# Final stage of a mixture-of-experts step: last block's act turned earlier, other blocks' sums added on TensorE, tiles normed one by one

## The reference

```
moe_ffn(h):      top_w, top_idx = softmax(top_4(h @ w_router + b_router))
                 for each block of up to 128 tokens of one expert:
                     g = min(h @ w_gate + b_gate, 7);  u = clip(h @ w_up + b_up, -7, 7)
                     a = (u + 1) * g * sigmoid(1.702 * g)
                     f[token] += top_w * (a @ w_down + b_down)
layer:           x = x + gate2 * f            (gate2: one row for the prompt, one per sample sequence)
output:          y = x * rsqrt(mean(x**2) + 1e-6) * g_final
```

## Time and profile before

| | |
|---|---|
| median of 3 runs (lowest, highest) | 1815.8 us (1811.48, 1818.57) |
| the profiled execution's own time | 1816.97 us |
| its span in the trace | 1815.2 us |
| TensorE busy | 1680.0 us, 93% of the span, 9012 instructions |
| VectorE busy | 1429.5 us, 79% |
| ScalarE busy | 1106.6 us, 61% |
| POOL busy | 330.1 us, 18% |
| moved by DMA | 516.08 MB, mean 284 GB/s |

### The profile page before, as it was taken

One profiled execution on the slowest core, in us unless ns is written; L12 is line 12 of the kernel. 1 busy time (PEld: TensorE's weight loads), 2 busy tenths in 40 slices (PEclk: granted clock), 3 DMA queues, 4 the chain that ended last, 5 costly groups with the idle time before them and its releaser, 6 DMA issues.

```text
span 1815.2 us, 27011 instructions
## 1 busy us (share of the span) xinstructions
PE 1680.0 (93%) x9012; PEld 1305.1 (72%) x9012; DVE 1429.5 (79%) x1357; ACT 1106.6 (61%) x1060; POOL 330.1 (18%) x310
## 2 busy tenths in 40 slices
PE   3999978788998779999999999999999999999994
PEld 2776767555554468888888888888888888888873
DVE  4422572576425879999999999999999999999996
ACT  4222342454434367777777777777777777777772
POOL 0000121300101012123122222312222231231110
PEclk9999989699998689999999999999999999999997
DMA  9454452610226479999999999999999999999973
GB/s 345 178 186 165 98 169 84 222 80 20 74 74 197 180 260 347 385 372 378 369 379 376 373 377 376 373 374 378 380 371 381 374 373 383 378 378 368 384 288 124
DMA packets 114598, 516.08 MB, mean 284 GB/s; under 512 B 25870, under 2 KB 47710, under 8 KB 62058
## 3 DMA queue, kind: packets, MB, share of 16 engines
q1 hardware_dynamic: 101082, 483.48, 70.6%
q0 software_dynamic: 12800, 29.45, 5.8%
q10 hardware_dynamic: 656, 2.36, 0.3%
HBM read 502.75 MB, written 31.09 MB: 294 GB/s over the span
## 4 chain that ended last, share of the span: by engine, by line
PE 61%; DVE 2%; ACT 1%; DMA 1%; issue 0%; DVEq 0%; POOL 0%; ACTq 0%; POOLq 0%
PE banks L2949 57%; PE banks L2957 3%; PE banks L2935 1%; DMA ffn_rows<-weighed,block_rows 0%; DVE arena L3220 0%; DVE arena L3219 0%; ACT sigmoids L3121 0%; DVE split L3142 0%; PE banks L3000 0%; ACT split L3053 0%; DMA arena<-ffn_rows 0%; DVE arena L3238 0%; DVEq L2816 0%; ACT final_stat L3122 0%; ACT L3127 0%
## 5 line engine op out<-in xcount | busy, mean ns | idle before, releaser
L2949 PE MATMUL banks<-split 128*128 128x512 f32 x4608 | 1077.3, 393 | 6.9 <-DVE split L3146 5.8
L2949 PEld LDWEIGHTS banks<-split 128*128 128x128 f32 x4608 | 861.2, 189 | 192.1 <-issue 13.2
L3142 DVE TENSOR_TENSOR split<-expert_buffers,split 128x2048 fp32r<-128x2048 f32 x384 | 864.4, 2284 | 41.4 <-ACT split L3053 39.8
L3053 ACT ACTIVATE split<-expert_buffers 128x2048 fp32r<-128x2048 f32 x384 | 732.9, 1918 | 217.7 <-PE banks L2949 213.3
L2888 POOL TENSOR_TENSOR wait_taken<-routing 128x1 f32<-128x1 f32 x62 | 76.5, 1234 | 808.9 <-PE banks L2957 464.1
L2911 POOL DMA_INDIRECT ffn_rows<-weighed,block_rows x31 | 107.7, 3476 | 4.8 <-issue 4.8
L662 PE MATMUL banks<-w_in_high,hT_high 128*128 128x476 f32 x192 | 75.6, 394 | 4.2 <-DVE hT_low L498 4.2
L3146 DVE TENSOR_TENSOR split<-banks,split 128x1024 fp32r<-128x1024 f32 x64 | 77.8, 1216 | 0.7 <-ACT split L3056 0.7
L662 PE MATMUL banks<-w_in_high,hT_low 128*128 128x476 f32 x192 | 72.9, 380 | 0.0
L3056 ACT ACTIVATE split<-banks 128x1024 fp32r<-128x1024 f32 x64 | 64.5, 1007 | 4.3 <-PE banks L2957 4.3
L3078 ACT ACTIVATE weighed<-banks,block_weights 128x1024 f32<-128x1024 f32 x32 | 35.8, 1117 | 45.3 <-PE banks L2949 45.3
(11 more groups left out here) (398 smaller groups left out, 1721.2 us busy)
## 6 DMA issues: line engine op xcount, KB each, us to landing
expert_buffers<-in_w_gate SPq DMA_DIRECT2D x128, 1024.0 KB, 8.0
expert_buffers<-in_w_up SPq DMA_DIRECT2D x128, 1024.0 KB, 18.9
expert_buffers<-in_w_down SPq DMA_DIRECT2D x128, 1024.0 KB, 8.5
arena<-in_w_ada SPq DMA_DIRECT2D x16, 1024.0 KB, 4.8
w_in_landing<-in_w_in SPq DMA_DIRECT2D x5, 1904.0 KB, 7.9
arena<-in_w_ada SPq DMA_DIRECT2D x4, 2048.0 KB, 20.6
arena<-in_x_prompt SPq DMA_DIRECT2D x8, 512.0 KB, 9.7
arena<-in_cache_cmp SPq DMA_DIRECT2D x32, 128.0 KB, 2.9
```

The source lines that it names most:

```text
L2949: last = pe.matmul(ps[:, bank + c, :], x[:, kt * P:(kt + 1) * P].bitcast(F32R), wt.bitcast(F32R), start=(m == 2 and kt == 0 and x is xs[0] ...
L3053: act.activation(high[:, j % RING_Q].bitcast(F32R), v, ACT.Copy).then_inc(s_high, 1)
L3142: dve.tensor_tensor(rest[:, j % RING_Q].bitcast(F32R), v, high[:, j % RING_Q], ALU.subtract).then_inc(s_rest, 1)
```

## The change

Five things change, all in `experts`:

1. **Act 31 is turned between the second and third quarter of down(30)** instead of behind it. Its split goes into `xh`, `xl`, ahead of the later quarters in ScalarE's and VectorE's queues, and down(31) writes the banks `GB` instead of `DB`.
2. **POOL takes the last block's rows and weights early**, into tiles of their own, before its last two adds. `hot` no longer waits for the add of block 30.
3. **TensorE adds the loaded sums**: for the four prompt tiles two float32 products with the identity matrix follow those with `hot`, in the same banks. The sample tile's sums are added by VectorE. The products with `hot` take `last_y` as it is; gate2 comes afterwards, once for each tile.
4. **The tiles are finished one by one**: Sqrt by ScalarE for a tile, reciprocal by VectorE, and one VectorE operation for scale and `g_final`. Ln, Exp and the two tiles of ScalarE are gone.
5. **Each tile is stored as soon as it is finished**, in the order 4, 0, 1, 2, 3.

```diff
@@ SP
-            for i, t in enumerate((FINAL[4], FINAL[0], FINAL[3], FINAL[1], FINAL[2])):
+            for i, t in enumerate(FINAL):
                 t0, n = TILES[t]
-                sp.wait_ge(s_oa if t in BY_ACT else s_o, i // 2 + 1)
+                sp.wait_ge(s_o, i + 1)
@@ POOL, behind the loop
+            pool.tensor_tensor(last_row, core.row_of[:, bass.ds(nb1, 1)], none, ALU.add).then_inc(s_lastrow, 1)
+            pool.tensor_tensor(last_weight, core.weight_of[:, bass.ds(nb1, 1)], none.bitcast(F32), ALU.add).then_inc(s_lastrow, 1)
             for n, done in ((nb2, nb3), (nb1, nb2)):
                 take_row(n, done)
                 add_rows(n, done)
-            take_row(nb, nb1)
@@ TensorE
-                product(2, (ah, al), DB, before)
+                product(2, (ah, al), DB, before, range(2))
+                if last:
+                    pe.wait_ge(s_a, nb)
+                    turn(u, s_atp)
+                product(2, (ah, al), DB, before, range(2, 4))
...
-            pe.wait_ge(s_a, nb)
-            turn(u, s_atp)
-            down(nb, nb1, first_of(nb1))
+            pe.wait_ge(s_at, nb)
+            product(2, (xh, xl), GB, first_of(nb1))
...
+            def other_rows(t):
+                pe.wait_ge(s_f[t], 16)
+                for c in range(2):
+                    last = pe.matmul(ps[:, BANK[t] + c, :], ident, f[:, t, c * 512:(c + 1) * 512], start=False, stop=True)
+                return last
 
             pe.wait_ge(s_hot, NT)
             pe.wait_ge(s_y, nb)
-            last_rows(ST, y)
-            pe.wait_ge(s_yg, 1)
+            last_rows(ST).then_inc(s_last, 1)
             for t in range(ST):
                 if t == 3:
                     pe.wait_ge(s_read, 1)
-                last_rows(t, yg)
+                last_rows(t)
+                other_rows(t).then_inc(s_last, 1)
@@ ScalarE
+            def weigh_last():
+                act.wait_ge(s_used, first_of(nb1) + 4)
+                act.wait_ge(s_lastrow, 2)
+                act.activation(last_y, ps[:, GB:GB + 2, :].rearrange("p b n -> p (b n)"), ACT.Copy, scale=last_weight
+                               ).then_inc(s_y, 1)
...
-                for j in range(3):
+                high_part(0, k)
+                if last:
+                    act.wait_ge(s_atp, nb)
+                    rounded(xh, s_ah)
+                for j in range(1, 3):
                     high_part(j, k)
...
-            link(act.activation(row, one, ACT.Ln))
+            link(act.activation(row, one, ACT.Sqrt))
             for i, t in enumerate(FINAL):
                 n = TILES[t][1]
                 act.wait_ge(s_x, i + 1)
                 link(act.activation(junk[0:n, :], x[0:n, t, :], ACT.Square, accum_out=stat[0:n, t:t + 1]))
-                act.activation(stat[0:n, NT + t:NT + t + 1], stat[0:n, t:t + 1], ACT.Ln, scale=1.0 / D,
-                               bias=eps[0:n, :]).then_inc(s_ln, 1)
...
+                act.activation(stat[0:n, NT + t:NT + t + 1], stat[0:n, t:t + 1], ACT.Sqrt, scale=1.0 / D, bias=eps[0:n, :]
+                               ).then_inc(s_rms, 1)
@@ VectorE
-                for j in range(4):
+                rest_part(0, k)
+                if last:
+                    rest_T(xh, xl, s_ah, nb, s_at)
+                for j in range(1, 4):
                     rest_part(j, k)
...
+            def sum_up(i, t):
                 n = TILES[t][1]
+                ft, gate = f[0:n, t, :], gate2[0:n, int(t == ST), :]
+                if t == ST:
+                    dve.wait_ge(s_f[ST], 16)
+                    dve.tensor_tensor(ft, ft, added(i, t), ALU.add).then_inc(s_read, 1)
+                    dve.wait_ge(s_read, 1)
+                    link(dve.tensor_tensor(ft, ft, gate, ALU.mult))
+                else:
+                    link(dve.tensor_tensor(ft, added(i, t), gate, ALU.mult))
+                dve.tensor_tensor(x[0:n, t, :], x[0:n, t, :], ft, ALU.add).then_inc(s_x, 1)
+
+            def finish(i, t):
+                n = TILES[t][1]
+                rstd = stat[0:n, NT + t:NT + t + 1]
+                dve.wait_ge(s_rms, i + 1)
+                link(dve.reciprocal(rstd, rstd))
+                dve.scalar_tensor_tensor(f[0:n, t, :], x[0:n, t, :], rstd, gfin[0:n, :], ALU.mult, ALU.mult).then_inc(s_o, 1)
...
             for i, t in enumerate(FINAL):
+                sum_up(i, t)
+                if i == 1:
+                    dve.wait_ge(s_gf, 16)
+                if i >= 1:
+                    finish(i - 1, FINAL[i - 1])
+            finish(NT - 1, FINAL[NT - 1])
```

More of the change, by code:

```diff
@@ L2768, in experts @@
     row_out, weight_out = own("block_rows", 1).bitcast(I32), own("block_weights", 1)
+    last_row, last_weight = own("last_block_rows", 1).bitcast(I32), own("last_block_weights", 1)
     g, u, s, y = (own(name, D) for name in ("gates", "ups", "sigmoids", "weighed"))
@@ L2785, in experts @@
     f = Stack(core, core.z_late, ARENA - N_SPLIT).take(NT * D).rearrange("p (t d) -> p t d", t=NT)
-    gfin, hot, junk, yg = xg, g[:, 0:NTOK], s, u
-    stat, row, rowf, rowt = own("final_stat", 2 * NT), own("ln_before", 1), own("last_rows", 1), own("last_rows_by_tile", NT)
+    gfin, hot, junk, last_y = xg, g[:, 0:NTOK], u, s
+    stat, row, rowf, rowt = own("final_stat", 2 * NT), own("root_loaded", 1), own("last_rows", 1), own("last_rows_by_tile", NT)
     FINAL = [ST] + list(range(ST))
-    BY_ACT = FINAL[0:2]
     BANK = {ST: GB, 0: UB, 1: TB, 2: DB, 3: GB}
     s_f = [core.sem(f"sums_in{t}") for t in range(NT)]
[L2792 to L2796, removed]
+    s_gf, s_hot, s_last, s_read = (core.sem(n) for n in (
+        "g_final_in", "last_rows_marked", "last_rows_ps", "last_rows_read"))
+    s_x, s_rms, s_o, s_out, s_act = (core.sem(n) for n in (
+        "x_final", "root_mean_square", "out_ready", "out_stored", "act_p7"))
+    s_lastrow = core.sem("last_block_taken")
     s_sum = [core.sem("gather_allowed"), core.sem("add_allowed")]
@@ L2935, in start_with_bias, with product @@
                     pe.matmul(ps[:, bank + c, :], ones[r0:r0 + 3, :], bias[r0:r0 + 3, :], start=True, stop=False)
-            def product(m, xs, bank, before):
-                for q in range(4):
+            def product(m, xs, bank, before, some=range(4)):
+                for q in some:
                     j = 4 * m + q
@@ L2984, in turn_act, with down @@
                 turn(u, s_atp)
-            def down(n, done, before):
+            def down(n, done, before, last=False):
                 pe.wait_ge(s_at, n)
@@ L3018, in step @@
                     turn_rows(k + 1)
-                down(k, prev, first_of(prev) + 8)
+                down(k, prev, first_of(prev) + 8, last)
             step(1, 0)
@@ L3024, in _, with last_rows @@
             step(nb1, nb2, last=True)
-            pe.wait_ge(s_a, nb)
-            turn(u, s_atp)
-            down(nb, nb1, first_of(nb1))
-            def last_rows(t, src):
+            pe.wait_ge(s_at, nb)
+            product(2, (xh, xl), GB, first_of(nb1))
+            def last_rows(t):
                 t0, n = TILES[t]
                 for c in range(2):
-                    last = pe.matmul(ps[0:n, BANK[t] + c, :], hot[:, t0:t0 + n], src[:, c * 512:(c + 1) * 512], start=True, stop=True)
-                last.then_inc(s_last, 1)
+                    last = pe.matmul(ps[0:n, BANK[t] + c, :], hot[:, t0:t0 + n], last_y[:, c * 512:(c + 1) * 512], start=True,
+                                     stop=(t == ST))
+                return last
[3 more added lines that the diff above has]
+                    last = pe.matmul(ps[:, BANK[t] + c, :], ident, f[:, t, c * 512:(c + 1) * 512], start=False, stop=True)
+                return last
             pe.wait_ge(s_hot, NT)
             pe.wait_ge(s_y, nb)
-            last_rows(ST, y)
-            pe.wait_ge(s_yg, 1)
+            last_rows(ST).then_inc(s_last, 1)
             for t in range(ST):
@@ L3112, in _ @@
             step(nb1, nb2, last=True)
-            acts_T(nb)
-            weigh(nb, nb1, first_of(nb1) + 4)
+            weigh_last()
             link = linker(act, s_act)
-            link(act.activation(row, one, ACT.Ln))
+            link(act.activation(row, one, ACT.Sqrt))
             for i, t in enumerate(FINAL):
@@ L3211, in _, with added @@
             step(nb1, nb2, last=True)
-            rest_T(ah, al, s_ah, nb, s_at)
             link = linker(dve, s_dve, dve_count)
-            def fold(t):
+            def added(i, t):
+                dve.wait_ge(s_last, i + 1)
+                return ps[0:TILES[t][1], BANK[t]:BANK[t] + 2, :].rearrange("p b n -> p (b n)")
+            def sum_up(i, t):
                 n = TILES[t][1]
[L3218 to L3223, removed]
+                ft, gate = f[0:n, t, :], gate2[0:n, int(t == ST), :]
[13 more added lines that the diff above has]
+                dve.scalar_tensor_tensor(f[0:n, t, :], x[0:n, t, :], rstd, gfin[0:n, :], ALU.mult, ALU.mult).then_inc(s_o, 1)
+            dve.wait_ge(s_lastrow, 2)
```

(5 more changed lines are left out.)

10 lines of the change are left out of this document (removed).

## The result

The changed kernel takes 1808.85 us (median of 20 runs, 1802.71 to 1814.95) against 1817.8 us before (20 runs, 1811.48 to 1820.89). The ratio is 0.9947, 95% interval 0.9938 to 0.9957: 9.6 us less, 7.8 to 11.3. The forecast was 7.3 us less, and 1808.5 us.

What follows compares the result with a forecast made beforehand. The end was bound by the chain through the add of block 30, sums' loads, VectorE's folds, norms and scaling. Gains of 5.0 us to VectorE's end and 2.3 in stores made 7.3, 1815.8 to 1808.5 us; range 1803.5 to 1815.5.

Steps and rivals of the forecast that it cites:

- The turn and the clock: Down(30) and down(31): no idle time, down(31) in 10.87 us, ending 7.8 us earlier; add of block 30 delayed 1.05 us.
- Rows taken early: Before POOL's last adds: two tiny POOL operations and VectorE's `hot` in 2.2 us, both while waiting, costing nothing.
- Sums on TensorE: End stage: identity products with `hot` products take 3.62 us a tile, TensorE keeping ahead of VectorE by about 1.1 us.
- `g_final`: VectorE's first finish: the load lands at 1788.45 and VectorE waits 0.8 us, a wait new on the path.
- VectorE: End stage: tiles 3.78 us apart, VectorE ending at 1802.9 instead of 1807.86, 5.0 us gained.
- The root: Norms: Exp's 1.28 us load and the wait of all for all go; Sqrt takes 0.30 us, its load hidden.
- C: Rival, norms: Square not in Sqrt's table, two loads of 1.28 us a tile; 1812.1 us, chance 0.05.
- D: Rival, end stage: TensorE's clock falls and stays, a tile takes 7.24 us; 1819.5 us, chance 0.06.
- B: Rival: add or sums 1 to 2 us later, TensorE bounds, or last store takes 4.3; gain 3 to 4.5, chance 0.15.
- A: Rival: turn nearly hidden, waits for `g_final` and tile 0's sums vanish (0.8 + 0.4 us); gain 9.5, 1806.3 us, chance 0.12.
- The stores: End of kernel: four of five leave while VectorE works, the last takes 2.8 us plus 2.1 to 2.3 ending; 2.3 us gained.

Runs made afterwards that it cites:

- e7: Changed kernel with all sums first and all five finishes last in VectorE's order; 48.5 us from act 31 to the end against 47.6, ratio to before 0.9963.
- e3: Changed kernel without the identity products, VectorE adding the prompt tiles' sums again; 51.2 us from act 31 to the end against 47.6, ratio to before 0.9988.
- e5: Changed kernel with `g_final` loaded before the wait for the add of block 30; 46.3 us from act 31 to the end against 47.6, ratio to before 0.9944.
- e2: Kernel before with only the early turn of act 31; 57.1 us from act 31 to the end against 55.8, ratio to before 1.0003.
- e1: Changed kernel with act 31 turned behind all of down(30) again; 53.1 us from act 31 to the end against 47.6, ratio to before 0.9999.
- e10: Changed kernel with a short hole in VectorE's queue before the third of the last block's four rests; 45.3 us from act 31 to the end, ratio to before 0.9954.
- e8: Changed kernel with the turn of act 31 made twice; 46.2 us from act 31 to the end against 47.6, ratio to before 0.9963.
- e9: Changed kernel with a short hole in VectorE's queue before the last quarter's rest; 45.4 us from act 31 to the end, ratio to before 0.9953.

## Why the prediction was right, point by point

The mechanism held, and so did most of the terms; the agreement of the level, 1808.5 against 1808.85 us, is partly luck. The forecast started from the 1815.8 us of three runs, and twenty runs gave 1817.8; it then took off 7.3 us where the ratio says 9.6, with an interval (7.8 to 11.3) that leaves 7.3 out. The two errors cancel. The gain of 0.53% (0.43 to 0.62) also lies on the border of the 0.5% within which the prediction put it with a chance of 0.69.

- **The turn and the clock**: down(31) without a gap at clock 1.00, as said. TensorE's end of down(31) went from 25.4 to 17.6 us behind the act, 7.8 earlier, as predicted. The price on the add's chain: `weigh` of block 30 from 5.88 to 6.91 us behind the act, 1.03 against 1.05.
- **Rows taken early**: cost nothing, as said; `hot` was ready 4.6 us before its use. That the part is worth something is an estimate: in the kernel before `hot` was ready 2.7 us behind the landing of the add of block 30 (1776.58 to 1779.29), which here would be 1780.4, and TensorE began with it at 1778.62. No run had this part alone.
- **Sums on TensorE**: one tile's pair took 3.43 us in the steady stretch, predicted 3.62. TensorE was ready 2.3 to 3.1 us before VectorE took up tiles 1 to 3, predicted 1.1. Without the finishes between the sums VectorE would have to wait for it (e7). Worth 3.6 us (e3).
- **`g_final`**: the wait that the forecast called new on the path was there, 1.45 us against 0.8 predicted; it cost 1.3 (e5).
- **VectorE**: tiles 3.79 us apart (1789.08, 1792.86, 1796.65, 1800.44), predicted 3.78. Its end 4.8 us earlier against 5.0.
- **The root**: Sqrt took 0.29 us, its load 1.28 and hidden; no load within a tile. That Exp's load and the wait of all tiles for all are gone is read from the trace; no run had this part alone.
- **The rivals**: C is out (no load within a tile) and D too (clock 1.00 from 1783 to 1796). Of B nothing came: the add's chain moved by 1.03 us, TensorE stayed ahead, the last store landed in 2.6 us. A's 9.5 us lie nearer to the measured 9.6 than the forecast's 7.3, but not by its mechanism: the turn's price stood (1.03 us at `weigh`, 1.4 at the end in e2), and so did the wait for `g_final`. Only its 0.4 us for tile 0's sums were right, VectorE took them up without a wait.
- **The stores** are the term that was mis-sized: 2.3 us predicted, 3.4 measured. The prediction took the shortest landing (2.8) and added 2.1 to 2.3 us of ending, which it had counted from the end of the traffic near 1812.9. But a landing lies later than the end of its traffic, in the kernel before by 0.6 us: its last store, issued at 1808.3 and landed 5.2 us later, leaves 1.7 us for the ending, not 2.3. In the changed kernel the last store (issued 1803.4, landed 2.6 us later) leaves 1.3. So the step counted 0.6 us twice, the ending became 0.4 us shorter, and the landing was 0.2 us shorter than the row. With 2.6 and 1.3 us the sum would have been 8.4 us; the aligned traces show 8.2.

The aligned traces, with what is lost outside the span, give 7.8 us, at the lower edge of the ratio's 7.8 to 11.3. e1 is near an edge too: by its trace 2.7 us less than before in the span, so 2.3 in device time, where its ratio allows from 2.5 us less to 2.2 us more. Whether a kernel's code also shifts the time ahead of this stage by a us or two is open; each was profiled once.

## What to carry to other kernels

Moving an engine's work earlier is worth nothing while another chain ends last; here it paid 5.5 us together with the change that put the sums behind it, and cost 1.4 us alone. So price parts of a change in pairs, not one by one: the prices of the early turn (5.5), the sums on TensorE (3.6) and the early stores (5.7), each taken out of the whole, add up to 14.8 us, where the whole change gave 8.2. Before an end stage is reordered, ask of each load in it what it depends on: `g_final` needed nothing of the add, and cost 1.3 us by standing behind loads that did. To tell effects of a us in a kernel whose runs spread over 10, count from an event that all versions share.

## What the runs showed of the hardware

POOL's instructions waited until a VectorE subtraction of two SBUF tiles (128x2048, 2.29 us) that was already running had ended: 1.82 and 3.44 us in the changed kernel, against 0.19 us with VectorE idle (the first instruction, e10) and 1.55 us with VectorE idle or at one column (the second, e8 and e9). All 31 issuing instructions of the changed kernel took 3.44 to 3.49 us, and all 31 of the kernel before 3.44 to 3.52, so the wait is there in every block; in the chain that ended last only that of block 30 stands. An indirect add issued by POOL was held up by this like a computation. The other way round nothing was lost: a subtraction that started 0.35 us behind the issuing instruction took its usual 2.29 us (e9). The Trainium skill, SBUF — State Buffer, section "Who interferes with whom", tells of an exclusive lock between the two that goes to the one who starts first; by that rule the trace agrees for POOL's tensor operation that comes second, while VectorE's subtraction that came second in e9 wasn't blocked. The page goes on that descriptor generation isn't stalled by such a two-input VectorE operation, and calls the reason inferred; here the issuing instruction of an indirect add took 1.9 us longer beside it, so for this kind of DMA the measurement decides against that; whether it waits with reading its row numbers from SBUF or with the descriptors, no run shows.
